# Low parts of 27 down-projection weight chunks subtracted on GpSimd instead of VectorE

## What is computed

```python
act = jax.nn.silu(jnp.einsum("nd,edf->nef", xt, w1)) * jnp.einsum("nd,edf->nef", xt, w3)
act = act * comb[:, :, None].astype(act.dtype)
y = jnp.einsum("nef,efd->nd", act, w2)          # w2: 16 experts, 256 x 1024 each
```

```python
x = x + (jax.nn.silu(hf @ w_ffn_gate) * (hf @ w_ffn_up)) @ w_ffn_down
```

## Time and profile before

| what | before |
|---|---|
| median of three runs | 1134.08 us |
| span of the profiled execution | 1137.6 us |
| PE busy | 1060.5 us (93%) |
| PEld busy | 977.2 us (86%) |
| DVE busy | 656.7 us (58%) |
| ACT busy | 497.8 us (44%) |
| POOL busy | 50.6 us (4%) |
| mean granted TensorE clock | 0.954 of full speed |
| DMA | 155.99 MB, 137 GB/s |

### The profile page before, as it was taken

How to read it: one execution, slowest core, us unless ns; L and a number is a source line. 1 busy time by engine, 2 the same in 40 slices (tenths; PEclk the granted TensorE clock), 3 DMA queues, 4 the chain that set the end, 5 groups by cost and what they waited for, 6 DMA issues and landing times.

```text
span 1137.6 us, 16395 instructions
## 1 busy us (share of the span) xinstructions
PE 1060.5 (93%) x7177; PEld 977.2 (86%) x7177; DVE 656.7 (58%) x727; ACT 497.8 (44%) x592; POOL 50.6 (4%) x66
## 2 busy tenths in 40 slices
PE   6999889999787999999999969999999899999987
PEld 5988888989786989999999868889799799999966
DVE  4875782428766445555554566988546544444453
ACT  4566421224844434434434455446455444334351
POOL 3000512300001000000000000000000000000000
PEclk9999996979888889999999989999999899999989
DMA  7644300003144245555565534443423555555520
GB/s 234 201 149 151 99 4 35 1 25 125 37 149 148 75 151 191 177 192 192 173 195 195 167 111 141 155 149 121 140 89 134 161 182 186 185 188 183 186 74 37
DMA packets 115645, 155.99 MB, mean 137 GB/s; under 512 B 5892, under 2 KB 92277, under 8 KB 115574
## 3 DMA queue, kind: packets, MB, share of 16 engines
q1 hardware_dynamic: 114838, 154.63, 41.5%
q10 hardware_dynamic: 736, 0.32, 0.1%
HBM read 153.89 MB, written 1.05 MB: 136 GB/s over the span
## 4 chain that ended last, share of the span: by engine, by line
PE 81%; DVE 9%; ACT 7%; issue 2%; DMA 0%; ACTq 0%; DVEq 0%
PE ps L864 13%; PE ps L866 13%; PE ps L865 13%; PE ps L880 9%; PE ps L881 8%; PE ps L882 8%; PE ps L1057 2%; DVE w_lo L1406 2%; PE ps L1070 2%; ACT w_hi L460 2%; PE ps L1066 2%; PE ps L1289 1%; PE ps L892 1%; PE ps L1241 1%; PE ps L1196 1%
## 5 line engine op out<-in xcount | busy, mean ns | idle before, releaser
L1406 DVE TENSOR_TENSOR w_lo<-raw,w_hi 128x2048 fp32r<-128x2048 f32 (+1 forms) x146 | 333.6, 2287 | 277.3 <-ACT w_hi L460 276.3
L864 PE MATMUL ps<-h_hi,w_hi 128*128 128x256 f32 x1280 | 367.9, 287 | 1.6 <-DVE h_lo L1415 1.6
L865 PE MATMUL ps<-h_lo,w_hi 128*128 128x256 f32 x1280 | 365.8, 286 | 0.0
L866 PE MATMUL ps<-h_hi,w_lo 128*128 128x256 f32 x1280 | 365.6, 286 | 0.0
L460 ACT ACTIVATE w_hi<-raw 128x2048 fp32r<-128x2048 f32 (+1 forms) x146 | 276.7, 1898 | 82.2 <-PE ps L882 75.0
L864 PEld LDWEIGHTS ps<-h_hi,w_hi 128*128 128x128 f32 x1280 | 249.6, 195 | 4.9 <-issue 3.7
L865 PEld LDWEIGHTS ps<-h_lo,w_hi 128*128 128x128 f32 x1280 | 249.6, 195 | 0.9
L866 PEld LDWEIGHTS ps<-h_hi,w_lo 128*128 128x128 f32 x1280 | 249.4, 195 | 0.0
L880 PE MATMUL ps<-w_hi,h_hi 128*128 128x512 f32 (+1 forms) x240 | 95.4, 398 | 2.7 <-DVE h_lo L1738 2.1
L881 PE MATMUL ps<-w_lo,h_hi 128*128 128x512 f32 (+1 forms) x240 | 94.2, 392 | 0.0
L882 PE MATMUL ps<-w_hi,h_lo 128*128 128x512 f32 (+1 forms) x240 | 93.9, 391 | 0.0
(11 more groups left out here) (365 smaller groups left out, 1242.7 us busy)
## 6 DMA issues: line engine op xcount, KB each, us to landing
raw<-in_w_in SPq DMA_DIRECT2D x36, 1024.0 KB, 5.2
raw<-in_w_exp_gate SPq DMA_DIRECT2D x16, 1024.0 KB, 5.5
raw<-in_w_exp_up SPq DMA_DIRECT2D x16, 1024.0 KB, 5.3
raw<-in_w_exp_down SPq DMA_DIRECT2D x16, 1024.0 KB, 4.9
raw<-in_w_ffn_gate SPq DMA_DIRECT2D x11, 1024.0 KB, 5.3
raw<-in_w_ffn_up SPq DMA_DIRECT2D x11, 1024.0 KB, 5.3
raw<-in_w_ffn_down SPq DMA_DIRECT2D x11, 1024.0 KB, 5.0
raw<-in_w_out SPq DMA_DIRECT2D x8, 1024.0 KB, 5.0
```

The source lines that it names most:

```text
L864: pe.matmul(o, hi[:, k, cols], a_hi[:, k, :], start=(k == 0), stop=False)
L865: pe.matmul(o, hi[:, k, cols], a_lo[:, k, :], start=False, stop=False)
L866: last_mm = pe.matmul(o, lo[:, k, cols], a_hi[:, k, :], start=False, stop=(k == kt - 1))
L1406: dve.tensor_tensor(w_lo[:, j % SPL, 0:kt * n], raw[:, j % RAW, 0:kt * n], w_hi[:, j % SPL, 0:kt * n].bitcast(F32), sub).then_inc(w_ready, 1)
```

## The change

The low parts of all 27 down chunks (16 experts, 11 pieces of the dense part) are subtracted by GpSimd, with the same operands in the same form. GpSimd does them one after the other in its own program, after the router's selectors; each waits only for its own high part. DVE's `ahead` passes over these chunks, without a wait. They have a ready semaphore of their own, `w_ready_by_pool`; `ready(i)` gives for each chunk the semaphore and the count, and both PE ahead of a chunk and SP ahead of a load into the chunk's `raw` buffer wait by it. Lines further down move by 8 to 22 in the changed file.

```diff
+        DOWNS = [EXP[e][2] for e in range(N_EXP)], [FFN[e][2] for e in range(FF_PAIRS)]
+        ON_POOL = DOWNS[0] + DOWNS[1]
...
+        w_ready_pool = sem("w_ready_by_pool")
+
+        def ready(i):
+
+            n_pool = sum(j <= i for j in ON_POOL)
+            return (w_ready_pool, n_pool) if i in ON_POOL else (w_ready, i + 1 - n_pool)
...
                 if i >= RAW:
-                    sp.wait_ge(w_ready, i - RAW + 1)
+                    sp.wait_ge(*ready(i - RAW))
...
+            def lows_of(js):
+                for j in js:
+                    _, kt, n = chunks[j]
+                    pool.wait_ge(w_high, j + 1)
+                    pool.tensor_tensor(w_lo[:, j % SPL, 0:kt * n], raw[:, j % RAW, 0:kt * n],
+                                       w_hi[:, j % SPL, 0:kt * n].bitcast(F32), ALU.subtract).then_inc(w_ready_pool, 1)
+
+            lows_of(DOWNS[0])
+            lows_of(DOWNS[1])
...
-                pe.wait_ge(w_ready, i + 1)
+                pe.wait_ge(*ready(i))
...
                     _, kt, n = chunks[j]
+                    if j in ON_POOL:
+                        split_at[0] += 1
+                        continue
                     dve.wait_ge(w_high, j + 1)
```

## The result

The changed kernel took 1139.55 us, the median of 20 runs (1134.71 to 1143.26); the kernel before, run beside it, 1133.52 us, the median of 20 (1130.89 to 1140.67). The ratio is 1.0047, with a 95% interval from 1.0032 to 1.0062: about 5.3 us slower. That is within 1%, as forecast, but nine times the 0.6 us of the sum, and by its median just above the range's upper end of 1139.5 us.

A forecast was written before the change was run, and what follows sets the result against it. PE was taken to set the pace in both stages, with DVE half idle. All terms were 0 except +0.6 us at the experts' end, so the median 1134.08 becomes 1134.7 us, range 1130.0 to 1139.5.

The forecast's parts named there:

- the 0.6 us of the sum: All terms over the whole kernel added up: +0.6 us, all of it from the last expert's end.
- What bounds the kernel: In the experts and dense part PE sets the pace; less DVE work there buys at most 0.7 us.
- The price of a subtraction on GpSimd: Each of the 27 moved low parts takes GpSimd 4.7 us, between 4.2 and 5.1.
- Rival B: GpSimd's subtraction is much slower; from 9.3 us on PE waits at down chunks; chance 0.06 of going beyond 1%.
- Steady part: For 23 of the 27 low parts, GpSimd finishes 4.6 us before PE needs the chunk; term 0.
- SP's queue: The load into the freed raw buffer goes out 2.4 us later, with slack about 11 us; term 0.
- dense part: First piece has 8.1 us for 4.7; at the last, GpSimd overlaps a DVE product reading PSUM, not held; term 0.
- Experts 0 and 1: GpSimd's first low part holds up DVE's gate 2 low part, hidden behind ACT's evictions with 0.8 us cover; term 0.
- The end of the experts: GpSimd's last expert low part holds DVE's product with two SBUF inputs, on the path: +0.6 us.
- Rival D: The lock also holds DVE's product reading PSUM at both stages' ends, 1.4 us each: 1136.9 us; chance 0.02.
- the 0.58 us come out whole: +0.6 us: At the last expert's end the chain to PE has no slack, so DVE's 0.58 us delay is paid in full.

The follow-up runs named there:

- dense_only: Changed kernel with only the dense part's 11 low parts on GpSimd, all experts' on VectorE; 1134.38 us against 1133.14 for the kernel before, ratio 0.9998.
- early_o_lo_pool: Changed kernel, with VectorE making the product's low part before the next stage's first low part at the last expert and dense piece; 1133.27 us, ratio 0.9983 to before.
- early_o_lo: Kernel before, with VectorE making the product's low part before the next stage's first low part at the last expert and dense piece; 1133.83 us, ratio 0.9977.
- only_last: Kernel before with one low part on GpSimd, that of the last expert's down chunk; 1139.86 us against 1133.14, ratio 1.0036.
- delay_end: Kernel before with a VectorE addition of 300 scratch elements, about 0.4 us, between the last expert's two products; 1140.36 us against 1133.14, ratio 1.0048.
- delay_norm1: Kernel before with a VectorE addition of 300 scratch elements in the norm ahead of the experts; 1139.66 us against 1135.28, ratio 1.0031.
- keep_last: Changed kernel with the last expert's low part kept on VectorE, the other 26 on GpSimd; 1136.49 us against 1133.14 for the kernel before, ratio 1.0025.
- keep_last_2: The kernel of keep_last timed once more on another chip; 1136.34 us against 1135.60 for the kernel before, ratio 1.0008.
- the first four experiments: keep_last, only_last, delay_end and dense_only, timed on one chip, where the kernel before has a median of 1133.14 us.
- delay_norm: Kernel before with a VectorE addition of 300 scratch elements in the norm behind the experts, ahead of the reciprocal; 1138.08 us against 1135.28, ratio 1.0016.
- delay_1us: Kernel before with a VectorE addition of 960 scratch elements, about 1.1 us, between the last expert's two products; 1139.78 us against 1135.60, ratio 1.0045.

## Why the prediction was right and wrong

**What bounds the kernel: right.** PE is busy throughout both steady parts, before and after, and 58.8 us less work on DVE moved nothing.

**The price of a subtraction on GpSimd: right.** 4.62 us for the 4.7 that I took from bounds of 4.2 and 5.1. Rival B, which needed 9.3 us, is out. The Trainium skill's 4497 ns ("GPSIMD Engine Reference", Performance versus the Vector engine) is 3% under the measured one.

**Steady part, SP's queue, dense part: right**, each at 0. dense_only shows it for the dense part by itself, and early_o_lo_pool beside early_o_lo for all 27 together, to about 0.2%.

**Experts 0 and 1: right.** Gate 2's low part was to be held up and was (DVE's timeline):

```profile
396.53 4.53 DVE L1428 TENSOR_TENSOR w_lo<-raw,w_hi 128x2048 fp32r<-128x2048 f32 x1 [3.40 <-ACT w_hi L479]
```

4.53 instead of 2.29 us, and it stayed hidden. GpSimd had started at 394.30 and ended at 398.92; DVE's operation needed 2.1 us more from there.

**The end of the experts: right in place and direction of the contact, and roughly in its size.** 0.40 us for 0.58: the subtraction took 0.08 us less, and once GpSimd was done, at 645.62, the product needed 0.55 us more (to 646.17), not its full 0.69. Rival D is out, the product that reads PSUM was not held. The rule of the Trainium skill ("SBUF — State Buffer", SBUF: two separate sides) is borne out by both places, but for some 0.15 us that the held operation has behind it when GpSimd is done.

**The failed step is the sentence "the 0.58 us come out whole: +0.6 us".** It prices a delay at its own length and stops. What follows is a gap of PE, in which the clock falls, and the low stretch is 7 us long before and 14 us after. That costs 2.2 us more, for which the sum has no term. It does not end there. In every profile with 0.80 behind the experts (eight of them, with the changed kernel) the clock at the dense part's start is 0.90 or 0.85. With 0.90 behind the experts it is 0.95 in three of four; the fourth is the execution of before that was profiled. Against the profile of dense_only, the changed kernel loses at the start of the dense part another 0.5 and 1.65 us, and 0.2 and 2.3 us at the last norm and behind it.

The mean clock over a whole run is on record for all runs of the experiments and of the changed kernel: it was 0.948 to 0.952 in all 20 runs of the changed kernel and in all 12 each of only_last, delay_end and delay_norm1, but in only 22 of 90 runs of the kernel before and in 9 of 36 of keep_last, keep_last_2 and dense_only, whose others have 0.954 to 0.960. This mean does not give the time by itself: early_o_lo_pool has 0.952 in 7 of its 12 runs, and its ratio is 0.9983.

**Where the 5.3 us are.** 0.4 us are the contact, 2.2 us the first low stretch; both are shown, by the traces and by only_last and delay_end. The rest, some 2.7 us, is put down to the later low stretches, long in more of the runs than before; this part is argued from profiles of single executions, not shown. Beside the first four experiments 16 of 35 runs of the kernel before lie between 1130.7 and 1131.5 us and others reach 1139.4, so it probably has the long later stretches in some runs as well, while no run of the changed kernel is under 1134.7. How often each stretch is long was not counted.

**What stays open.** 0.4 us more make the stretch longer, and 1.85 us less (early_o_lo) do so too. In all twelve profiles this goes with how long after the fall PE begins again, so with when the gap comes against the clock's own course and not with its length alone; but no run here moves the one against the other by itself, and what sets the moment of the fall is not shown. Nor is it known how often the stretch is short or long in the runs that have no profile here: delay_norm, long in its profile, has 4 of 12 runs with a mean clock of 0.958 to 0.961, and of the six kernels with a later restart and the long stretch it is the only one whose ratio can't be told from 1. early_o_lo's median is 1.8 us lower although its stretch is the long one. One of its 12 runs took 1128.02 us, 3.1 us less than the next, and may be one that has both, no wait and the short stretch; it has no profile.

## What to carry to other kernels

A delay in front of a gap of the bounding engine must be priced with what the gap does to the clock, not at its own length: here 0.4 us became about 5, and an added operation of 1.1 us gave about the same. Read for it when the clock falls in the gap and how long after that the engine begins again; a stall taken away can end in the longer low stretch as well. Before moving work to an idle engine, look for the one place where its longer run meets a two-input operation on the path; that last iteration of the loop is where the slack ends, and keeping it on the old engine, or taking the chain behind it off the path, is worth more than the move. When an experiment adds an instruction, compare the whole trace behind it, since the engine's later pauses may have moved.

## What the runs showed of the hardware

- TensorE's low stretches behind the experts and at the start of the dense part were about 3.5, 7, 10.5 or 14 us long in the windows of 35 us. Behind the experts it was 7 us where PE began again 3.8 to 4.1 us after the fall (four profiles) and 14 us where it was 4.2 to 5.5 us (eight). PE's restart came 0.4 us later against the end of the experts' up chunks in the changed kernel, only_last, delay_norm and delay_norm1, 0.7 in delay_end and 1.4 in delay_1us, and all six have the long stretch.
- DVE has pauses of about 0.35 us between two instructions that wait for nothing in the profile, and in the three kernels with one instruction more in its program ahead of it, in delay_norm1 300 us ahead, such a pause stood on the path.
- A DVE operation with two SBUF inputs that meets a GpSimd subtraction ends later, 4.53 for 2.29 us and 1.09 for 0.69 us, and the wait shows as its own longer duration, not as idle time. Even a small one: the 300 scratch elements of delay_norm1, which fell beside GpSimd's selectors, took 2.17 us, and 0.47 us in delay_norm.
